# Two projection pieces in the second step of each layer's first attention kind

## The reference, cut to what matters

```python
u = rms_norm(h, ln_mix[l])
(aq, ak, av, bq, bk, bv, cq, ck, cv, dq, dzf, dzb, di, dg, gz) = split_in(u @ w_in[l])
y_a = windowed_sink_attention(...)
y_b = axial_rope_attention(...)
y_c = differential_attention(...)      # a = softmax(s0) - lam * softmax(s1)
y_d = hgrn2_bidirectional(...)
```

## Time and profile before

| | us |
|---|---|
| median of 3 runs | 3038.37 |
| lowest, highest | 3037.96, 3038.71 |
| profiled execution | 3040.5 |
| its span | 3038.7 |
| PE busy in the span | 2971.1 (98%) |
| DVE busy | 1749.4 (58%) |
| ACT busy | 1007.4 (33%) |

### The profile page before, as it was taken

One profiled execution on the slowest core, in us unless ns is written; L12 is line 12 of the kernel. 1 busy time (PEld: TensorE's weight loads), 2 busy tenths in 40 slices (PEclk: granted clock), 3 DMA queues, 4 the chain that ended last, 5 costly groups with the idle time before them and its releaser, 6 DMA issues.

```text
span 3038.7 us, 52919 instructions
## 1 busy us (share of the span) xinstructions
PE 2971.1 (98%) x22196; PEld 2597.3 (85%) x22196; DVE 1749.4 (58%) x3412; ACT 1007.4 (33%) x1772; POOL 216.5 (7%) x446
## 2 busy tenths in 40 slices
PE   8999999999999999999999999999999999999998
PEld 8877999999999997789999788887888875788887
DVE  5564577547647347557755774746537555743334
ACT  4655233232212236543323221224222324532222
POOL 0130222000000010312210000000000000000000
PEclk9999999999999999999999999999999999999999
DMA  5201111244534331111123453522324331213232
GB/s 193 102 28 37 53 62 62 72 145 159 172 109 131 112 117 43 46 53 60 64 70 143 151 189 105 173 97 84 120 95 140 130 109 39 84 58 107 86 105 76
DMA packets 75588, 302.54 MB, mean 100 GB/s; under 512 B 10793, under 2 KB 13225, under 8 KB 70361
## 3 DMA queue, kind: packets, MB, share of 16 engines
q1 hardware_dynamic: 58968, 230.04, 23.1%
q0 software_dynamic: 16384, 69.13, 6.4%
HBM read 288.51 MB, written 14.63 MB: 100 GB/s over the span
## 4 chain that ended last, share of the span: by engine, by line
PE 89%; DVE 4%; ACT 4%; issue 2%; DMA 1%; POOL 0%; SPq 0%; DVEq 0%; ACTq 0%; POOLq 0%
PE acc L1141 18%; PE acc L1142 18%; PE acc L1143 18%; PE acc L1592 5%; PE acc L1593 5%; PE acc L1594 5%; ACT temps L2087 2%; PE acc L1467 1%; PE acc L1408 1%; PE acc L1176 1%; PE acc L1830 1%; PE acc L1637 1%; PE acc L1658 1%; PE acc L1314 1%; PE acc L1441 1%
## 5 line engine op out<-in xcount | busy, mean ns | idle before, releaser
L1142 PE MATMUL acc<-normed_r,toep_r 128*128 128x512 f32 (+2 forms) x1792 | 620.6, 346 | 0.0
L1954 ACT ACTIVATE toep_r<-ring 128x1024 fp32r<-128x1024 f32 (+2 forms) x332 | 384.2, 1159 | 617.9 <-PE acc L1143 617.9
L2511 DVE TENSOR_TENSOR ring_r<-ring,toep_r 128x1024 fp32r<-128x1024 f32 (+2 forms) x332 | 448.0, 1350 | 243.1 <-ACT toep_r L1954 242.6
L1142 PEld LDWEIGHTS acc<-normed_r,toep_r 128*128 128x128 f32 x1792 | 336.7, 188 | 42.8 <-issue 0.2
L1141 PE MATMUL acc<-work_r,toep_r 128*128 128x512 f32 (+2 forms) x1076 | 357.4, 332 | 0.1
L1143 PE MATMUL acc<-work_r,ring_r 128*128 128x512 f32 (+2 forms) x1076 | 355.6, 331 | 0.0
L1141 PE MATMUL acc<-mixed_r,toep_r 128*128 128x264 f32 (+1 forms) x1056 | 342.7, 325 | 0.1
L1143 PE MATMUL acc<-mixed_r,ring_r 128*128 128x264 f32 (+1 forms) x1056 | 338.8, 321 | 0.0
L1142 PE MATMUL acc<-work_r,toep_r 128*128 128x512 f32 (+2 forms) x968 | 322.2, 333 | 0.0
L1592 PE MATMUL acc<-residual_r,toep_r 128*128 128x264 f32 (+1 forms) x1024 | 300.6, 294 | 3.7 <-ACT toep L2234 2.1
L1593 PE MATMUL acc<-normed_r,toep_r 128*128 128x264 f32 (+1 forms) x1024 | 291.9, 285 | 0.0
(11 more groups left out here) (456 smaller groups left out, 5410.4 us busy)
## 6 DMA issues: line engine op xcount, KB each, us to landing
ring<-in_w_pair SPq DMA_DIRECT2D x172, 512.0 KB, 3.5
ring<-in_w_down SPq DMA_DIRECT2D x64, 704.0 KB, 4.1
ring<-in_w_gb SPq DMA_DIRECT2D x64, 640.0 KB, 3.9
extra<-in_w_ada POOLq DMA_DIRECT2D x18, 1024.0 KB, 6.0
toep<-in_w_ada POOLq DMA_DIRECT2D x18, 1024.0 KB, 5.8
ring<-in_w_tm SPq DMA_DIRECT2D x24, 512.0 KB, 4.5
ring<-in_w_out SPq DMA_DIRECT2D x24, 512.0 KB, 3.6
ring<-in_w_fm SPq DMA_DIRECT2D x20, 512.0 KB, 4.0
```

The costliest lines, as they stand in the source:

```text
L1142: mm(out, wh, xl[:, a:z], start=False, stop=False)
L1954: A(high(ld), slot(ld), ACT.Copy).then_inc(S["w_high"], 1)
L2511: V.tensor_tensor(low(ld), slot(ld), high(ld), ALU.subtract).then_inc(S["w_low"], 1)
```

## The change

The pieces of kind C move forward by one place from the third piece on: steps 0, 1, 1, 2, ... instead of 0, 1, 2, 3, ... . Step 1 has two pieces, the last step of C none, and the places in A and B stay. In a step with several pieces all but the last are now issued ahead of `turn_probs(att[n-1], 0)`. ACT's and DVE's code is unchanged, but it follows the same places: in a step with two pieces ACT copies both one after the other, where it copied one. No instruction is added or removed.

```diff
             if ly["l"] == 0:
-                places_of = [c0 + i for i in range(10)] + [a0 + i for i in (1, 2, 4, 5, 7, 8, 9)] + [b0 + i for i in range(6)]
+                places_of = [c0 + i for i in (0, 1, 1, 2, 3, 4, 5, 6, 7, 8)] + [a0 + i for i in (1, 2, 4, 5, 7, 8, 9)] + [b0 + i for i in range(6)]
             else:
-                places_of = [c0 + i for i in range(8)] + [a0 + i for i in range(8)] + [b0 + i for i in range(6)]
+                places_of = [c0 + i for i in (0, 1, 1, 2, 3, 4, 5, 6)] + [a0 + i for i in range(8)] + [b0 + i for i in range(6)]
...
+                    pieces = fills_at.get(n, ()) if n < end else ()
+                    for f in pieces[:-1]:
+                        fill_piece(f)
                     if first <= n - 1 < end:
                         turn_probs(att[n - 1], 0)
                         if second_bank(n - 1) != 4:
                             turn_probs(att[n - 1], 1)
-                    for f in fills_at.get(n, ()) if n < end else ():
+                    for f in pieces[-1:]:
                         fill_piece(f)
```

## The result

The changed kernel takes 3062.76 us (median of 4 runs, 3061.75 to 3067.52), the one before 3038.54 us (4 runs, 3037.96 to 3039.62): the ratio is 1.0084, with a 95% interval of 1.0073 to 1.0096. It is 24.2 us slower, where 18.2 were forecast.

What follows compares the result with a forecast made beforehand. The prediction took a DVE-ACT loop to bound kind C, with PE beside it. Bank wait 7.2, split 6.2, last step -0.3 and clock 5.1 made 18.2 us on 3038.4, giving 3056.6 us, range 3046.5 to 3066.

Steps and rivals of the forecast that it cites:

- What bounds C: Kind C: a loop between DVE and ACT sets the pace, PE runs beside it with 0.6 us slack in step 1.
- First piece: Step 1 of C: it goes into PE's 1.74 us idle hole and alone costs nothing.
- Second piece: Step 1 of C: waits for ACT's copy of the piece before it, 3.6 us late per layer, 7.2 for both.
- The split: Layer 0 step 4, layer 1 step 3: a piece waits for DVE's low part of its weights; 2.7 and 3.5, together 6.2 us.
- From scores to use: Steps of C: 1.64 us from the start of PE's scores to DVE's first use of them.
- The last step: End of C: the removed piece leaves a hole of about 2.5 us, not a gain; -0.3 us in all.
- The clock: PE behind the four new holes in C: the granted clock falls to 1.2 GHz; three falls taken, 5.1 us.
- falls at 1.7 us: Behind new holes in C: 3.4 us at 1.2 GHz loses 1.7 us each; two to four falls, chance 0.45.
- only the longest hole falling: Rival: only the 4.7 us hole in layer 1, step 3 brings a fall; 14.8 us, 3053.2; one fall, chance 0.16.
- heavier clock: Rival: falls behind all six holes in C, longer than 3.4 us; 3062 to 3066 us, chance 0.12.
- the forecast's case: Kind C, both layers: four waits and two to four falls of the clock; 3056.6 us, chance 0.45.

Runs made afterwards that it cites:

- e8_last_pieces_cut: The kernel before with the last piece of kind C cut to 3 of its 24 products in both layers; 3039.24 us, ratio 1.0002.
- e3_order_only: The kernel before, places unchanged, with the one piece of step 1 issued ahead of the first transposes in each layer; 3038.55 us, ratio 1.0006.
- e1_split_early: The changed kernel with the second weight group split one step earlier in both layers; 3049.93 us, ratio 1.0043 to the kernel before.

## Why the prediction was right, point by point

- **What bounds C.** Right. The order alone gave nothing (1.8, from -1.2 to 4.9) and 5.2 us less work for PE gave nothing.
- **First piece.** Right: it cost nothing in layer 0 and filled the hole, and it won nothing. What I had not seen is that the hole moves behind the transposes, where in layer 1 the order alone lost 0.6 us by a fall of the clock.
- **Second piece.** Right in cause and size: a wait of 3.02 and 3.03 us (3.1 forecast) and 3.4 and 3.3 us lost (3.6 forecast). Early copying took it away.
- **The split.** Right: waits of 3.38 and 4.29 us (3.4 and 4.7 forecast), 2.6 and 3.3 us lost (2.7 and 3.5 forecast). Splitting early took them away.
- **From scores to use.** A small error in all four: I took the 1.64 us of C's first step from the start of the scores to DVE's use. Behind the waits it is 1.52 (123.89 to 125.41), so each loss was put 0.12 us too high.
- **The last step.** No gain, as forecast; the -0.3 us can't be seen.
- **The clock.** The mechanism was right, and this is the term of the sum that was mis-sized: 5.1 us for three falls of 1.7. Six falls came, and five of them cost time, 2.59, 2.65, 1.44, 1.51 and 2.3 us, 10.5 us together. I had a slow stretch of 3.4 us from the one example before. Two of the new ones were of that length, and three lasted 6.8 us, like that from 116.9 to 123.7, so that a whole piece ran at 1.2 GHz. The trace of before held a longer one that I had not looked at, 10.2 us from 178.0 on, in the last step of layer 0's C. The two cases that I set against each other, falls at 1.7 us and only the longest hole falling, both fell short. What came was my own "heavier clock", falls behind all six holes and longer than 3.4 us, which I gave 0.12 against 0.45 for the forecast's case; its 3062 to 3066 held the measured time. The reason I gave for it didn't hold: the later holes were not longer for the falls before them (3.38 and 4.29 us, 3.4 and 4.7 forecast).

So of the 6 us between forecast and result, 5.4 are the clock, the -0.3 us of the last step didn't come, the waits were forecast 0.8 us too large, and 1.1 us lies outside C, less than executions differ there. How much of a loss is the wait and how much the clock is measured for the bank wait, by the order without a long hole; the last step's 2.3 us agree with the 2.4 by which the unread products bring A's second scores forward; for the split it is worked out from the piece's time in one trace.

The Trainium skill's rule on idle gaps ("TensorE: Matmul & The Clock Gate", section "HAM oscillation — how this bites in real kernels") would have had the clock fall behind the longest hole alone. The holes of 3.02, 3.03, 3.38 and 2.51 us show falls too, so here the measurement decides against it.

## What to carry to other kernels

A hole on an engine is worth filling only if that engine is on the path there: the chain cut to the stretch told it, the busy share of 98% did not. Before work is moved forward, list what it waits for and who else's queue that stands in; here one piece came to stand behind four exponentials and another ahead of its own weights. And when a move opens a hole on TensorE, look for all slow stretches in the trace, not for one example, and count the clock behind the hole at their lengths, the long ones included.

## What the runs showed of the hardware

- The clock fell in or behind every hole of 2.5 to 4.3 us in C and behind one of 2.15 us (e8_last_pieces_cut, layer 1), did not behind 1.74 and 1.32 us, and behind a hole of about 1.9 us fell in layer 1 (1.89) and not in layer 0 (1.88) of one execution (e3_order_only). A single hole of that length can't be called safe or unsafe from this. In the last step of layer 0's C the kernel before shows a fall at 178.0 with holes of only 0.48 us (in front of 177.74) and 1.03 us (in front of 179.27) nearby, so the length of a hole doesn't decide alone.
- The slow stretches in and behind C lasted 3.4, 6.8, 10.2 or 13.7 us in these traces, and the hole doesn't tell which: behind the same hole of 3.0 us in step 1 of layer 0 the clock was down for 6.8 us in both traces of the changed kernel and for 3.4 us in e1_split_early. One fall cost 1.4 to 1.5 us with a short stretch and 2.3 to 2.7 with a long one.
- Products that nobody reads, in a hole that can't be closed, made the kernel faster: 18.2 us over before instead of 24.9.
- An avoided fall can make the next one dearer or cheaper. With the unread products in step 1, step 2's scores of layer 1 came 1.43 us earlier than in the changed kernel, but those of step 4 only 0.57 us (37.31 against 37.88 after the start of C): the slow stretch at the split lasted 6.8 us instead of 3.4. In layer 0 it lasted 3.4 instead of 6.8, and 2.67 us at step 2 became 4.14 at step 5 (42.41 against 46.55).
